# Feed-forward weight sums: two of the eight adds of a step as accumulating transfers issued by GpSimd

## The reference, cut to what matters

```
h2 = rms_norm(x, g_norm2[l]) * (1 + sc2) + sh2
ffn = (jax.nn.silu(h2 @ w_gate[l]) * (h2 @ w_up[l])) @ w_down[l]
x = x + gt2 * ffn
...
y = _rms(h, norm_ffn_g[i])
h = h + (jax.nn.silu(y @ w_gate[i]) * (y @ w_up[i])) @ w_down[i]
```

## Time and profile before

| | kernel before |
|---|---|
| runs, us | 2290.09, 2290.84 (median 2290.47) |
| profiled execution, us | 2287.8 |
| its span, us | 2286.1 |
| TensorE (PE) matmul busy | 2232.5 us, 98% |
| VectorE (DVE) busy | 1895.9 us, 83% |
| ScalarE (ACT) busy | 1163.9 us, 51% |
| GpSimd (POOL) busy | 86.5 us, 4% |
| PE's share of the chain that ended last | 79% |

### The profile page before, as it was taken

The page is one execution under the profiler, slowest core; times in us unless marked ns, Lnnn a source line. Parts: engine busy times, 40 slices in busy tenths (PEclk is TensorE's granted clock), DMA queues, the critical chain, the costliest instruction groups (busy, mean ns, idle before and its releaser), DMA issues.

```text
span 2286.1 us, 30531 instructions
## 1 busy us (share of the span) xinstructions
PE 2232.5 (98%) x10404; PEld 1788.6 (78%) x10404; DVE 1895.9 (83%) x2267; ACT 1163.9 (51%) x1465; POOL 86.5 (4%) x116
## 2 busy tenths in 40 slices
PE   6999989999999999999999999999999999999997
PEld 3577657788888888888888887888888888888886
DVE  4376877989988888999895998589889999999866
ACT  3233466465545555555545444555555555555554
POOL 1100030000000000000020000000000000000020
PEclk9999999999999999999999999999999999999999
DMA  9999995856656656666656564666556666656564
GB/s 391 414 362 373 406 358 191 322 208 206 194 192 202 199 194 197 200 201 202 203 175 220 176 185 165 194 218 202 194 193 200 196 200 210 197 186 205 187 200 147
DMA packets 131565, 518.23 MB, mean 227 GB/s; under 512 B 14496, under 2 KB 20256, under 8 KB 118304
## 3 DMA queue, kind: packets, MB, share of 16 engines
q1 hardware_dynamic: 121552, 449.11, 59.1%
q0 software_dynamic: 9216, 67.11, 7.2%
q10 hardware_dynamic: 720, 0.99, 0.1%
HBM read 512.96 MB, written 4.19 MB: 226 GB/s over the span
## 4 chain that ended last, share of the span: by engine, by line
PE 79%; DVE 4%; issue 1%; DMA 1%; ACT 1%; DVEq 0%; ACTq 0%
PE ps L2429 55%; PE ps L2610 19%; DVE w_lo L1906 1%; PE ps L2417 1%; PE ps L2574 1%; PE ps L2823 1%; DVE gate L2175 1%; PE ps L2895 0%; DMA raw<-in_w_in 0%; PE ps L2798 0%; PE ps L2797 0%; DMA raw<-in_w_out 0%; ACT w_hi L887 0%; PE ps L2813 0%; DVE stage L1895 0%
## 5 line engine op out<-in xcount | busy, mean ns | idle before, releaser
L887 ACT ACTIVATE w_hi<-raw 128x1024 fp32r<-128x1024 f32 (+1 forms) x498 | 514.8, 1051 | 451.0 <-PE ps L2610 249.3
L1906 DVE TENSOR_TENSOR w_lo<-raw,w_hi 128x1024 fp32r<-128x1024 f32 (+1 forms) x248 | 299.6, 1218 | 151.4 <-ACT w_hi L887 146.4
L887 ACT ACTIVATE w_hi_more<-raw 128x1024 fp32r<-128x1024 f32 x264 | 278.9, 1056 | 212.3 <-DMA raw<-in_w_down 112.9
L2610 PE MATMUL ps<-w_lo,fm_hi 128*128 128x512 f32 (+1 forms) x896 | 346.7, 387 | 0.0
L2610 PE MATMUL ps<-w_hi,fm_hi 128*128 128x512 f32 (+1 forms) x840 | 331.5, 395 | 6.2 <-DVE w_lo L1906 2.9
L2429 PE MATMUL ps<-w_lo,fm_hi 128*128 128x512 f32 x800 | 311.3, 389 | 0.0
L2610 PE MATMUL ps<-w_hi,fm_lo 128*128 128x512 f32 (+1 forms) x776 | 299.6, 386 | 0.0
L1589 DVE TENSOR_TENSOR w_lo<-raw,w_hi_more 128x1024 fp32r<-128x1024 f32 x240 | 287.8, 1220 | 7.1
L1589 DVE TENSOR_TENSOR w_lo<-raw,w_hi 128x1024 fp32r<-128x1024 f32 x240 | 284.5, 1220 | 4.0
L2429 PE MATMUL ps<-w_lo,hid_hi 128*128 128x512 f32 x640 | 249.0, 389 | 0.0
L803 ACT ACTIVATE sum_w_hi<-sum_raw 128x1024 fp32r<-128x1024 f32 x120 | 126.9, 1057 | 173.7 <-DVE sum_raw L1616 121.1
(11 more groups left out here) (370 smaller groups left out, 3792.6 us busy)
## 6 DMA issues: line engine op xcount, KB each, us to landing
raw<-in_w_gate SPq DMA_DIRECT2D x176, 512.0 KB, 4.3
raw<-in_w_up SPq DMA_DIRECT2D x176, 512.0 KB, 3.6
raw<-in_w_down SPq DMA_DIRECT2D x176, 512.0 KB, 3.7
ada_raw<-in_w_ada POOLq DMA_DIRECT2D x64, 1024.0 KB, 10.7
raw<-in_w_in SPq DMA_DIRECT2D x120, 512.0 KB, 3.8
raw<-in_w_out SPq DMA_DIRECT2D x64, 512.0 KB, 3.7
ada_raw<-in_w_ada SPq DMA_DIRECT2D x16, 1024.0 KB, 7.6
ada_raw<-in_w_gate SPq DMA_DIRECT2D x16, 1024.0 KB, 5.5
```

Of the source, the lines that this page charges most:

```text
L887: act.activation(hi_tile(like)[:, :, 0:width], raw[:, slot, :, 0:width], ACT.Copy).then_inc(hi_ready, 1)
L1906: dve.tensor_tensor(w_lo[:, slot, :, 0:width], raw[:, slot, :, 0:width], hi_tile(p)[:, :, 0:width], ALU.subtract).then_inc(lo_dve, 1)
L2610: last = pe.matmul(banks[t][:, 0:width], a, b, start=kt == 0 and k == 0, stop=kt == kts - 1 and k == 2)
```

## The change

The sum v is no longer made by VectorE. GpSimd gets a loop of its own, `pool_ffn`, once in each feed-forward part: for each step and group it waits until the sum u stands (u reads b12, which v overwrites), and then issues a transfer that reads the b22 piece from HBM a second time and adds it to b12 in its `raw` slot, while it lands. Its landing raises `v_summed[k]`, for which ScalarE's high part of v now waits. VectorE's `sum_v` is gone from `early` and `middle`, and in `middle` the sum u of group 1 stands two operations earlier: ahead of the low part of z 0 instead of behind the low part of c 3. The constants of `form_summed` go from 4 to 3 sums per group.

```diff
-SUMMED = (("u", 0), ("v", 0), ("w", 0), ("z", 0), ("u", 1), ("v", 1), ("w", 1), ("z", 1))
+SUMMED = (("u", 0), ("w", 0), ("z", 0), ("u", 1), ("w", 1), ("z", 1))
...
             def piece_hi(i, kind, k):
 
                 if kind == "v":
-                    act.wait_ge(form_summed, (i + before) * 4 * GROUPS + SUMMED.index((kind, k)) + 1)
+                    act.wait_ge(v_summed[k], i * 16 + (before + 1) * 16)
                 split_body(i, a, 24, (at_piece(kind, k),))
...
+        def pool_ffn(pool, name, u_view, done):
+
+            a, before = FIRST[name] + 2 * UP, FFN_STEPS - 1 if done else 0
+            with pool.Fori(0, FFN_STEPS - 1) as i:
+                for k in range(GROUPS):
+                    part, j = step_source(at_piece("b22", k))
+                    slot = (a + at_piece("v", k)) % RAW
+                    pool.wait_ge(form_summed, (i + before) * 3 * GROUPS + SUMMED.index(("u", k)) + 1)
+                    pool.dma_start(raw[:, slot, :, :], weight_tile(u_view[1:], i, j, NW), accum_op=ALU.add).then_inc(v_summed[k], 16)
+
         def pool_block2(pool, rests, rest_loop):
+            pool_ffn(pool, "ffn1", io["w_up"], 0)
             pool.wait_ge(settled, 1)
...
-            def sum_v(i, k):
-
-                b12, b22 = at_piece("v", k), at_piece("b22", k)
-                landed(i, b22)
-                dve.tensor_tensor(piece_raw(b12), piece_raw(b12), piece_raw(b22), ALU.add).then_inc(form_summed, 1)
-
...
-            def early(i, hook, hook_first=False):
+            def early(i, hook):
 
                 sum_u(i, 0)
                 piece_low(i, "b11", 0)
                 piece_low(i, "c", 0)
-                if hook_first:
-                    hook()
-                sum_v(i, 0)
-                if not hook_first:
-                    hook()
+                hook()
                 sum_w(i, 0)
...
                 sum_low(i, "w", 0)
                 piece_low(i, "b21", 0)
+                sum_u(i, 1)
                 sum_low(i, "z", 0)
                 piece_low(i, "c", 3)
-                sum_u(i, 1)
                 piece_low(i, "b11", 1)
-                sum_v(i, 1)
                 sum_w(i, 1)
```

More of the change, by code:

```diff
@@ L459, in build @@
         form_summed, form_hi, form_lo, form_used = sem("form_summed"), sem("form_hi"), sem("form_lo"), sem("form_used")
+        v_summed = [sem("v_summed0"), sem("v_summed1")]
         sub_rstd = sem("sub_rstd")
@@ L799, in sum_hi @@
             def sum_hi(i, kind, k):
-                act.wait_ge(form_summed, (i + before) * 4 * GROUPS + SUMMED.index((kind, k)) + 1)
+                act.wait_ge(form_summed, (i + before) * 3 * GROUPS + SUMMED.index((kind, k)) + 1)
                 q = sum_place(kind, k)
@@ L1172, in pool_block2 @@
             pool.tensor_tensor(mix_lo[:, 4:8, :], part[:, 0, :, :], mix_hi[:, 4:8, :], ALU.subtract).then_inc(part_lo, 1)
+            pool_ffn(pool, "ffn2", io["w_up_2"], FFN_STEPS)
             rests(FIRST["ple_g"], LO_PLE)
@@ L1593, in sum_low @@
                 q = sum_place(kind, k)
-                dve.wait_ge(form_summed, (i + before) * 4 * GROUPS + SUMMED.index(("z" if kind == "w" else "w", k)) + 1)
+                dve.wait_ge(form_summed, (i + before) * 3 * GROUPS + SUMMED.index(("z" if kind == "w" else "w", k)) + 1)
                 dve.wait_ge(form_hi, (i + before) * 3 * GROUPS + USED.index((kind, k)) + 1)
@@ L1601, in summed @@
             def summed(i, kind, k):
-                dve.wait_ge(form_summed, (i + before) * 4 * GROUPS + SUMMED.index((kind, k)) + 1)
+                dve.wait_ge(form_summed, (i + before) * 3 * GROUPS + SUMMED.index((kind, k)) + 1)
             def place_free(i, kind, k):
@@ L1640, in piece_low @@
             def piece_low(i, kind, k):
-                needed = {"b11": "u", "v": "v", "b22": "w", "b21": "z"}.get(kind)
+                needed = {"b11": "u", "b22": "w", "b21": "z"}.get(kind)
                 if needed:
@@ L1666, in first_lows @@
             def first_lows(i):
-                early(i, hidden_first, True)
+                early(i, hidden_first)
             def middle(i):
```

## The result

The changed kernel takes 2448.6 us in the median (2445.8 and 2451.4), against 2290.5 before: a ratio of 1.069, 95% interval 1.064 to 1.074. That is 158 us slower, where 54 were predicted, and above the top of the range (2420). The sign and the place of the loss are as forecast; its size is not.

What follows compares the result with a forecast made beforehand. TensorE was taken to bound the kernel; late landings of v cost 20 x (2 x 6.4 - 10.1) = 54 us, with VectorE's relief, extra traffic and clock at 0, giving 2344 us against 2290.5; range 2289 to 2420 us.

Steps and rivals of the forecast that it cites:

- What bounds: Whole kernel: TensorE's matmuls alone set the time, so VectorE's relief and the extra traffic are worth 0.
- The budgets of 5.1 and 5.0 us: Time from the end of sum u to the latest harmless landing: 5.1 us in group 0, 5.0 in group 1.
- the formula: Each step grows by (L - 5.1) + (L - 5.0) if v is late; 20 steps cost 20 x (2L - 10.1).
- L: Time from the end of sum u to the landing of the accumulating transfer in a feed-forward step; taken as 6.4 us.
- The path: At v, ScalarE's high part waits for the DMA; VectorE keeping GpSimd from issuing was a rival, 2392 us, chance 0.04.
- the thin row and the busy one: GpSimd's single 1 MB loads before the change: landing after 5.1 us at 81% DMA activity, 7.4 at 101%.
- TensorE's clock: Feed-forward loops: gaps of 1.4 us shouldn't lower TensorE's clock, so it stays at 1.00 and costs 0.
- Equal groups: Feed-forward steps: one L of 6.4 us for both groups, with waits of about 1.3 to 1.4 us each.
- late as forecast or more: Rival at v's landing: L from 6.2 to 8.3 us, time 2336 to 2420 us, chance 0.42.
- very late: Rival at v's landing: L = 8.9 us as in GpSimd's busy stretch, 154 us more, 2444 us, chance 0.07.
- In time: Rival at v's landing: L at most about 5.05 us, so not slower, 2290 us, chance 0.27.

Runs made afterwards that it cites:

- e1: The change without its transfers: GpSimd issues nothing in the feed-forward parts and nobody adds b22 to b12; 2290.3 us, ratio 1.000 against the kernel before.
- e7: Kernel before with all sums on VectorE, sum u of group 1 moved up, plus the 40 accumulating transfers onto a spare tile nobody reads; 2289.6 us, ratio 0.9995.
- e11: The change with the sum u of group 1 back in its old place, two VectorE operations later; 2473.1 us, ratio 1.080 against the kernel before.
- e9: e7 with plain loads of the same 512 KB to the spare tile instead of accumulating transfers; 2287.2 us.
- e2: The change in group 0 alone, v of group 1 made by VectorE again; 2348.3 us, ratio 1.024 against the kernel before.
- e3: The change in group 1 alone, v of group 0 made by VectorE again; 2413.6 us, ratio 1.052 against the kernel before.
- e4: The change with plain loads in place of the accumulating ones, so b22 overwrites b12; 2358.0 us, ratio 1.029 against the kernel before.
- e8: The change with group 0's v accumulated in its own tile a step ahead, group 1's v by VectorE; 2292.0 us, ratio 1.0006 against the kernel before.
- e13: The changed kernel itself, run once more; 2440.2 us, ratio 1.064 against the kernel before.
- e6: The change with half of each v sum by transfer (256 KB) and half by VectorE; 2383.3 us, ratio 1.040 against the kernel before.

## Why the prediction was wrong

Right steps, each with what shows it:

- *What bounds.* TensorE alone; a relief of VectorE is worth 0 (e1), the extra traffic 0 with the share at the 0.71 to 0.72 foreseen (e7).
- *The budgets of 5.1 and 5.0 us and the formula, nearly.* In the step shown they make waits of 1.94 and 3.73 us, and it has 1.65 and 3.55. Over all steps L is 7.41 in group 0 and 8.96 in group 1 in the mean, so 20 x (2.31 + 3.96) = 125 us, where 113 stand in the row of waits and 119 are lost. All 40 waits stand at v, none at what is queued behind it, and nothing is carried into the next step.
- *The path.* ScalarE's waits ahead of the high part of v are for the DMA. GpSimd's issue is not held up by VectorE: it is 0.88 in every case and begins within VectorE's operation of 611.86. e11 confirms the direction of the move, at 33 us instead of 46.
- SyncE's loads still land in 3.6 us in the median (533 to 1170 us), though one took 8.6.

Failed steps:

- **The term L.** "Between 5.1 and 7.4 the middle is 6.25; I take 6.4 with a hand-over on GpSimd". L is 7.41 in group 0 and 8.96 in group 1 in the mean, 7.04 and 8.73 in the step shown. The sizes were mis-set in three places: the hand-over to GpSimd is 0.64 where 0.15 was allowed; the issue is 0.88, not the fixed 0.54 that I had read off plain loads; and from there to the landing it is 5.5 and 7.2 in the step shown. Plain loads of twice the bytes in the earlier trace rows were a poor stand-in: the addition costs 3.4 us on top of a plain tile of the same size (e7 against e9). Of the middle between the thin row and the busy one, 6.25, nothing spoke for the lower half. The waits cost 119 us instead of 54: 65 of the 110 us that were missing between the two profiled executions; 8 of the others aren't the change's. Yet by the formula the measured L gives 2415 us, inside the range.
- **TensorE's clock: 0.** "it waited up to 11.9 us for a load and the clock of the page's slices stayed at nine tenths or more, so gaps of 1.4 us shouldn't lower it". The clock cost some 35 us behind the waits, and this took the time over the upper end. For gaps of 1.4 the conclusion stands (no wait under 1.8 us brought a fall), but neither piece of evidence bore it. Slices of 57 us round away a short stretch at half speed; the changed kernel's read nine tenths throughout as well. And the 11.9 us are the time from the span's start to TensorE's first matmul. The eight matmuls behind it took 1.94 us, where the same eight took 1.06 later, so TensorE may well have run at its lower level there; the trace's record of the granted clock begins only at 23.6 us. The two rows, of the kernel before:

```profile
11.93 1.94 PE L2646 MATMUL ps<-ada_raw,c_wide 128*32 128x512 f32 x8 [11.93 <-DMA ada_raw<-in_w_ada]
...
25.42 1.06 PE L2646 MATMUL ps<-ada_raw,c_wide 128*32 128x512 f32 x8
```

- **Equal groups.** One L was taken for both. e2 and e3 show 2.2 and 4.05 us of wait, so the loss is mostly group 1's.

So waits of 1.3 to 1.4 us were forecast and are 2.0 and 3.6 in the mean; steps of 66.2 us and are 71.4; a clock of 1.00 in the loops and it is 0.98. VectorE's share, 0.77 instead of 0.84, is the same work in longer steps.

The rival that holds by its condition is *late as forecast or more*: the mean L of both groups is 8.2, near its upper end. That *very late*, to which I gave 0.07, is near in time is luck: its L = 8.9 gives 154 us, near the 158, but by waits alone. The real loss is smaller waits and a slower TensorE behind them. *In time* needed L = 5.05: only plain tiles in group 0 came to that, with 5.1 in the median (e4).

## What to carry to other kernels

Work that is moved to another engine or queue has to be priced by its latency at the place where it is read, not by the time it frees: here VectorE had nothing to give, and v had 5 us between the moment its inputs stood and its need. An accumulating transfer is nearly twice as long as a plain one of the same size; it is harmless only where there is slack for its whole latency, up to 10 us here (e8), and a gain would need an engine that is waiting for VectorE, which no run here tried. Where TensorE sets the time, a wait of about 2 us or more in a full stream can cost more than its length, here 1.7 us or more for each fall of the clock, and the granted clock must be read in stretches as short as the wait.

## What the runs showed of the hardware

- GpSimd's accumulating transfer, at a DMA share of 0.6 to 0.7: issue 0.88 us instead of 0.54 for a plain one, whatever its size; landing 7.8 us for 512 KB and 5.4 for 256 KB, instead of 4.4 plain for 512 KB; engine time 3.2 us instead of 1.6.
- From the end of the instruction that GpSimd waits for to the start of the issue: 0.64 us, where ScalarE starts 0.03 us after the same sum (611.77 behind 611.74).
- TensorE's clock behind short waits in a full stream, over the 216 waits at v in the changed kernel, e13, e11, e2, e3, e4 and e6: it fell to the lower level at none of 47 waits under 1.8 us, at 27 of 64 between 1.8 and 2.4, at 28 of 34 up to 3.2, at 19 of 22 up to 3.6, and at all 49 longer ones. The length of the wait alone doesn't decide: in the changed kernel it fell at a wait of 1.9 us and not at one of 2.65 (the row at 836.1).
- A transfer of GpSimd in the same kernel can land 2 us later at one place of the step than at another (6.8 and 8.7 us in e7, where nobody waits for it).
